# Two more seven-product pairs in the first and last feed-forward layer, and conditioning blocks placed anew

## What is computed

```python
def _swiglu(h, w13, w2):
    a, b = jnp.split(h @ w13, 2, axis=-1)
    return (jax.nn.silu(a) * b) @ w2

m = jax.nn.silu(cvec) @ ada_w[l] + ada_b[l]     # 9 vectors of D per layer
x + 0.5 * m[gate] * _swiglu(_modulate(x, m, s, g), w13, w2)
```

## Time and profile before

| | us |
|---|---|
| median of 3 runs | 3096.23 (3092.04 to 3099.06) |
| the profiled execution | 3098.46 |
| its span, first to last instruction | 3096.4 |
| PE busy / PEld busy | 2959.1 / 2722.7 |
| DVE busy / ACT busy / POOL busy | 2005.0 / 1135.8 / 275.6 |
| mean granted TensorE clock | 0.988 of full speed |

### The profile page before, as it was taken

One profiled execution on the slowest core, in us unless ns is written; L12 is line 12 of the kernel. 1 busy time (PEld: TensorE's weight loads), 2 busy tenths in 40 slices (PEclk: granted clock), 3 DMA queues, 4 the chain that ended last, 5 costly groups with the idle time before them and its releaser, 6 DMA issues.

```text
span 3096.4 us, 46067 instructions
## 1 busy us (share of the span) xinstructions
PE 2959.1 (96%) x18222; PEld 2722.7 (88%) x18222; DVE 2005.0 (65%) x3616; ACT 1135.8 (37%) x2024; POOL 275.6 (9%) x335
## 2 busy tenths in 40 slices
PE   7999999998999899999999999999999999999998
PEld 3999998988878899998999998878687886899998
DVE  3778977245756787887687766463545545667756
ACT  4223434335455233534343444222212222534433
POOL 1000002011003000003000003030301104100001
PEclk9999999999999899999999999999999999999999
DMA  5454342220101333342233222313223241122221
GB/s 220 135 176 126 107 133 90 81 70 26 41 15 62 116 123 122 107 126 94 71 116 116 91 92 89 116 64 98 96 70 122 69 135 41 41 89 89 79 80 67
DMA packets 87686, 294.42 MB, mean 95 GB/s; under 512 B 10512, under 2 KB 14896, under 8 KB 86704
## 3 DMA queue, kind: packets, MB, share of 16 engines
q1 hardware_dynamic: 80080, 269.70, 26.8%
q10 hardware_dynamic: 6176, 16.54, 1.4%
q0 software_dynamic: 1216, 5.24, 0.5%
HBM read 283.96 MB, written 7.49 MB: 94 GB/s over the span
## 4 chain that ended last, share of the span: by engine, by line
PE 84%; DVE 7%; ACT 3%; POOL 2%; issue 2%; DMA 1%; DVEq 0%; POOLq 0%; SPq 0%; ACTq 0%
PE ps L2147 24%; PE ps L2180 17%; PE ps L2313 12%; PE ps L2048 11%; PE ps L2063 7%; PE ps L2109 2%; PE ps L2585 2%; POOL tmp_q L647 2%; PE ps L2594 2%; PE ps L2370 1%; PE ps L2338 1%; DMA raw<-in_ws 1%; PE ps L2261 1%; PE ps L2573 1%; PE ps L2353 1%
## 5 line engine op out<-in xcount | busy, mean ns | idle before, releaser
L2180 PE MATMUL ps<-g,w 128*128 128x320 f32 x4224 | 625.4, 309 | 2.2 <-DVE w L1303 1.3
L2180 PEld LDWEIGHTS ps<-g,w 128*128 128x128 f32 x4224 | 620.6, 188 | 3.6 <-DVE w L1303 1.6
L2147 PE MATMUL ps<-h,w 128*128 128x320 f32 x3168 | 498.9, 312 | 43.5 <-ACT swu L950 29.2
L2147 PEld LDWEIGHTS ps<-h,w 128*128 128x128 f32 x3168 | 476.3, 190 | 49.1 <-ACT swu L950 31.6
L1303 DVE TENSOR_TENSOR w<-raw,w 128x1024 fp32r<-128x1024 f32 (+1 forms) x267 | 303.1, 1141 | 224.5 <-ACT w L798 206.9
L2313 PE MATMUL ps<-w,h 128*128 128x512 f32 x1620 | 374.5, 391 | 4.8 <-ACT rv L1239 3.1
L2147 PE MATMUL ps<-e,w 128*128 128x320 f32 x2376 | 371.8, 310 | 0.0
L2313 PEld LDWEIGHTS ps<-w,h 128*128 128x128 f32 x1620 | 302.3, 188 | 70.0 <-issue 6.8
L2147 PEld LDWEIGHTS ps<-e,w 128*128 128x128 f32 x2376 | 356.1, 189 | 0.0
L811 ACT ACTIVATE w<-w2s 128x512 fp32r<-128x512 f32 x264 | 164.1, 631 | 249.7 <-DVE w2s L1450 80.6
L2063 PE MATMUL ps<-h,w 128*128 128x320 f32 x1728 | 254.3, 309 | 0.2 <-DVE w L1303 0.2
(11 more groups left out here) (249 smaller groups left out, 3381.4 us busy)
## 6 DMA issues: line engine op xcount, KB each, us to landing
raw<-in_ws SPq DMA_DIRECT2D x303, 512.0 KB, 3.6
raw<-in_ada SPq DMA_DIRECT2D x128, 512.0 KB, 3.7
raw<-in_ws SPq DMA_DIRECT2D x96, 384.0 KB, 3.2
ada<-in_ada ACTq DMA_DIRECT2D x6, 1024.0 KB, 22.1
rst<-in_state ACTq DMA_DIRECT2D x4, 1024.0 KB, 4.8
out_new_state<-rsx ACTq DMA_DIRECT2D x8, 512.0 KB, 2.6
x<-in_xT SPq DMA_DIRECT2D x4, 640.0 KB, 8.0
ada<-in_ada POOLq DMA_DIRECT2D x2, 1024.0 KB, 16.2
```

What stands on the lines that cost most here:

```text
L2147: mm = pe.matmul(ps[:, 4 * s + bank, 0:HT], w2[:, at // 2, wi, c:c + P], rhs(k, ri), start=start and k + wi + ri == 0, stop=(k == 3 and wi ...
L2180: mm = pe.matmul(pair_half(pr, half), w2[:, slot_of(n), wi, c:c + P], half_of(g2[:, k, ri, :], half), start=k + wi + ri == 0, stop=(k == n ...
```

## The change

The number of plain pairs goes from 10 to 8 in FFN 0 and from 4 to 2 in FFN 3, and the T values of FFN 3 are made one pair earlier. The conditioning blocks are spread anew (128 in all as before, with those of the retention layer). The fourth T value gets a buffer of its own in all FFNs, so that FFN 0 uses the order of the others. In a seven-product pair ACT makes the first copy ahead of `left_high(nxt, 0)`, and DVE makes `left_first_sum` ahead of `first_half_low` and `left_low(nxt, 0)` after the conditioning blocks.

```diff
-CLASSIC = (10, 4, 4, 4)
-T_PAIR = (3, 1, 1, 1)
+CLASSIC = (8, 4, 4, 2)
+T_PAIR = (3, 1, 1, 0)
...
-ADA_UP = [[1, 3, 3, 0, 2, 3, 3, 3, 3, 0, 0, 1, 1, 0, 1, 1, 1, 0, 1, 0, 1, 0],
-          [1, 0, 3, 2, 1, 1, 1, 0, 1, 0, 1, 0, 1, 0, 1, 0, 1, 0, 1, 0, 1, 0], [0] * FT, [0] * FT]
-ADA_DN = [[6, 6, 6, 2], [6, 6, 6, 2], [6, 6, 0, 0], [0] * 4]
+ADA_UP = [[1, 3, 3, 0, 3, 2, 3, 2, 0, 1, 1, 0, 0, 1, 1, 1, 1, 0, 0, 1, 0, 0],
+          [1, 0, 3, 2, 0, 2] + [0] * 16, [1, 0, 3, 2, 0, 2] + [0] * 16, [0] * FT]
+ADA_DN = [[7, 7, 7, 3], [6, 6, 4, 0], [6, 6, 4, 0], [0] * 4]
...
+        fourth = place("fourth", 4 * HT, at=f_at + 5 * T * 4).rearrange("p (k t) -> p k t", k=4)
...
-        def fourth_value(q):
-
-            return tscr if q else e2s[:, 2, :, 0, :]
...
-            return t_first(q) + 1 + (v if q or v < 2 else 5 - v)
+            return t_first(q) + 1 + v
...
@@ ACT, first_pairs: the T values' high parts
-                    for v in range(3 if q else 2):
+                    for v in range(3):
                         t_high(q, v)
...
                 if f + 1 == CLASSIC[q] < FT:
                     t_high(q, 3)
-                    if q == 0:
-                        t_high(q, 2)
...
@@ ACT, seven_products
-                if not last:
-                    left_high(q, f + 1, n + 2, 0)
                 if u and f > CLASSIC[q]:
                     first_half_high(f - 1, u - 1)
+                if f == CLASSIC[q] + 1:
+                    act.wait_ge(t_lo, t_turn(q, 3))
                 act.wait_ge(left_free, 5 * sg + 1)
                 act.activation(swu[:, s, 0, :], ps[:, 4 * s, 0:HT], ACT.Copy).then_inc(p_copied, 1)
                 if last:
                     split_in(q, d)
+                else:
+                    left_high(q, f + 1, n + 2, 0)
                 act.wait_ge(left_free, 5 * sg + 2)
                 act.activation(swu[:, s, 1, :], ps[:, 4 * s + 2, 0:HT], ACT.Copy).then_inc(p_copied, 1)
...
@@ DVE, first_pairs: the T values' low parts (t_low(q, 2) moves from after t_low(q, 3) to T_PAIR in FFN 0)
...
@@ DVE, seven_products
                 if not last:
-                    left_low(*nxt, 0)
+                    left_first_sum(*nxt)
                 if before:
                     first_half_low(f - 1, u - 1)
-                if not last:
-                    left_first_sum(*nxt)
                 ada_blocks(ADA_UP[q][f])
                 if not last:
+                    left_low(*nxt, 0)
                     left_second_sum(*nxt)
```

More of the change, by code:

```diff
@@ L820, in t_high @@
                 act.wait_ge(t_val, t_first(q) + 1 + v)
-                if q == 0 and v == 2:
-                    act.wait_ge(t_lo, t_turn(q, 3))
                 if v < 3:
@@ L825, in t_high @@
                 else:
-                    act.activation(h2[:, 0:4, 0, HT:T], fourth_value(q), ACT.Copy).then_inc(t_hi, 1)
+                    act.activation(h2[:, 0:4, 0, HT:T], fourth, ACT.Copy).then_inc(t_hi, 1)
             def norm_sq(k, nn, ready, h=None):
@@ L1494, in t_values @@
                     low_done(dve, nn, 0, k)
-                dve.tensor_tensor(fourth_value(q), tscr, t2, ALU.subtract).then_inc(t_val, 1)
+                dve.tensor_tensor(fourth, tscr, t2, ALU.subtract).then_inc(t_val, 1)
             def t_low(q, v):
@@ L1507, in t_low @@
                 else:
-                    dve.tensor_tensor(h2[:, 0:4, 1, HT:T], fourth_value(q), h2[:, 0:4, 0, HT:T].bitcast(fp32), ALU.subtract
+                    dve.tensor_tensor(h2[:, 0:4, 1, HT:T], fourth, h2[:, 0:4, 0, HT:T].bitcast(fp32), ALU.subtract
                                       ).then_inc(t_lo, 1)
@@ L1545, in first_pairs @@
                     t_low(q, 1)
-                    if q:
-                        t_low(q, 2)
+                    t_low(q, 2)
                 if seven:
```

## The result

The changed kernel takes **3115.15 us** (median of 5 runs, 3112.75 to 3119.16) where the kernel before takes 3096.23: ratio **1.0057 [1.0046, 1.0069]**, slower by 18.9 us. The forecast was 3108.4 in a range of 3096 to 3120. The profiled execution took 3119.16 us with a span of 3117.4, 21.0 above the span before, at a mean granted clock of 0.981 (0.988 before). So kernels are compared by their medians, and places inside them by the traces.

What follows compares the result with a forecast made beforehand. PE work (busy 2959 of 3096 us) plus few stalls was taken as the bound. Terms -7.0 - 16.4 + 14.6 + 20.0 + 0.9 = +12.1 on 3098.5 gave 3110.6, less 2.2 a median of 3108.4 us; range 3096 to 3120.

Steps and rivals of the forecast that it cites:

- transition stall: PE's wait at product 3 of the first seven-product pair: FFN 2's pair 4, +12.5, and FFN 0's pair 8, +7.7.
- seventh block: Conditioning block in FFN 0's down tiles, m = 6: its late load holds DVE; pairs 12 and 18 lose +5.0 each.
- FFN 1, -16.4: FFN 1: pairs 6 to 21 lose all their blocks, pair 4 its own, the last down products two; -16.4 us in sum.
- FFN 2, +14.6: FFN 2 gets FFN 1's block pattern: pair 4 +12.5, pair 5 +0.9, the moved low part +1.2; +14.6 us in sum.
- FFN 0, pair 8, +7.7: FFN 0's first seven-product pair, now 8, repeats the stall of FFN 1's pair 4: loss 15.5 for 7.8, +7.7 us.
- The down gap, -1.6: FFN 0, pair 5 has two blocks for three: a 1.30 us wait in the down products goes, with its restart, -1.6.
- pairs 9, 10 and 13 to 16 of FFN 0, +1.9 forecast: FFN 0: a block each in pairs 9 and 10 costs +0.9, and one each in pairs 13 to 16 costs +1.0.
- DVE waits in each pair with a block: Rival, chance 0.13: the moved first sum may wait about 1 us in seven FFN 0 pairs; 3115 to 3117 us.
- The last down products of FFN 0, +2.0: FFN 0's last down products get a third block behind tile 2's add, 0 to 2.6 us, taken as +2.0.
- transition stall not back: Rival, chance 0.07: no stall at product 3 of FFN 2's pair 4 and FFN 0's pair 8, 20.2 less; 3088.2 us.
- seventh block hidden: Rival, chance 0.14: the load lands in time, FFN 0's pairs 12 and 18 stay as they are, 10.0 less; 3098.4 us.
- The fourth rival: Chance 0.02: the 48 matmuls saved are replaced by equal waits, as DVE has more to do in seven-product pairs; 3115.4 us.

Runs made afterwards that it cites:

- FFN 3's part alone: The kernel before with only FFN 3 changed: two plain pairs for four and the T values one pair earlier; 3094.44 us, ratio 0.9999.
- the last experiment: The changed kernel with six for seven blocks, both orders as before, low parts 5 and 6 ahead of blocks, ten plain pairs in FFN 0; 3078.15 us, ratio 0.9935.

## Why the prediction was right, and by how much it was off

The forecast was for slower by the coming back of the transition stall and by the seventh block, at +12.1 of trace; the trace has +21.0. Segment by segment the changed places sum to +18.7. The rest lies in places that no edit touches, most of it between FFN 2 and FFN 3: +2.8 in two stretches, of which 0.9 comes back before FFN 3 begins. Direction, range and mechanism were right. The median came 6.7 above the forecast, and one term is 9.0 too small; the others are off by 1.7 us or less each, together -2.4.

- **Four pairs, -7.0:** the matmuls went as told; the counts show it.
- **FFN 1, -16.4:** -17.2 in its pairs (rounds -1.7, -7.2, -4.7, -3.6) and -0.9 in the last down products, so -18.1. Rounds 1 to 3 came to 74.3, 74.9 and 49.3, within 1 us of 73.9, 73.9, 49.3. Pair 4 kept 14.1 of 16.8, 15.5 forecast. The copy moved ahead is not what gave more: with ACT's order as before the pair loses 14.4. With the tables of before it loses 16.7, so the whole gain goes with the new table.
- **FFN 2, +14.6:** +12.0, +0.6 and +0.2 in its rounds, +12.9. Pair 4 loses 14.4 (15.5 forecast), PE waits 12.38 there for ACT's copy as said ("12 to 13 us"), and 12.1 in pair 4 of FFN 1 and in pair 8 of FFN 0. The tables of before bring pair 4 of FFN 2 back to 2.7, and the low parts moved ahead of the blocks take 5.3 to 6.1 us off at each place: that two blocks ahead of the ring's release make the stall is shown, not only argued. How the 9 us that then stay divide between the work left ahead of low part 5 and the load's own time is read from the timeline alone.
- **FFN 0, pair 8, +7.7:** it loses 15.0 for pair 10's 7.7, so +7.3. The down gap, -1.6: it was -1.6.
- **The seventh block, +10.0:** pairs 12 and 18 lose 9.4 and 8.0 for 3.8 each, +9.8, by the chain as worked out: 3.7 from issue to use of the block, and PE 6.49 idle for 6.7 forecast (6.24 in pair 18). Taking the block out gave 12.7 in the median. Without it they lose less than the 3.8 of before, which fits with the block of their own that both pairs had then and have no more: in FFN 1 the same two pairs lose 1.0 and nothing without theirs, 4.4 and 3.6 with it.
- **The term that was too small: pairs 9, 10 and 13 to 16 of FFN 0, +1.9 forecast.** "A fourth is +1.0" took the price of such a pair from the old order. The pairs beside 8, 12 and 18 lose 12.8 for 1.9 of before, +10.9. The cost was in the text as the rival "DVE waits in each pair with a block", at about 1 us in each of seven pairs and a chance of 0.13. It should have been a term of the sum. Nothing excluded it: the prediction itself said that the load goes out only after low part 5, and put +0.6 a round on the moved low part in FFN 1 and 2, where it has no blocks to meet. What it also missed is the other half, ACT's high part behind a copy that waits for PE, which costs about the same alone. Undone together they give 8.1, and the pairs lose 4.9. The 3.0 that this is above the 1.9 of before goes with the new table, which gives four of these pairs a block that had none; it was not taken apart.
- **The last down products of FFN 0, +2.0:** +3.2 here (29.77 for 26.54). Among the nine others with the same three blocks it was 28.5 in three (+2.0), about 29.8 in five and 31.0 in one (both orders as before); why it differs is open.
- **FFN 3, +0.9:** +1.3, pair 2 loses 4.2 for 3.8 to 3.9 forecast.

The rivals "transition stall not back" and "seventh block hidden" fell by the first sight of the windows. The largest sum, 3115 to 3117, named with the DVE rival, is where the time came out. The fourth rival's 3115.4 is as near, but as the cause of the time it falls: FFN 3's part alone keeps about 2.1 of its 3.5 in the trace. In FFN 0 it holds in part, since there, by the last experiment, the two pairs bring nothing.

The estimate from the Trainium skill ("DMA: Bandwidth & Descriptors", "Anatomy of one DMA — SWDGE (gpsimd) path"), 3.2 us for 512 KB, would have put the sum 3.5 lower. The rows above have 3.5 to 3.7 from issue to use, so the trace is the better price here, as the loads go another issuing path.

## What to carry to other kernels

Where one ring of buffers feeds several engines that run their programs in order, find the operation that releases a place and look at what stands ahead of it: moving it ahead of two optional blocks at three places gave 14.3 us, while moving the waiting copies gave nothing in the median. An operation that needs a load just issued is not free to move earlier by a place, even on an engine that is 65% busy: it stops all that is behind it. And price a moved operation with the order it will stand in, not with the rows of the old one.

## What was not expected

- Two causes that hide each other. By the medians, DVE's order undone alone gave 1.7 us, ACT's alone lost 0.6, and both together gave 8.1. Either run by itself would have called the order free.
- A stall costs more than its wait. In pair 4 of FFN 2 the wait was 12.38 and the loss 14.4; the product behind it took 3.57 where 1.92 is usual, and the granted clock is 0.74 in the window of the pair:

```profile
1512.30:1539.00 26.70, 14.32 (x86) 14.06 (x85) 20.20 (x34) 10.54 (x19) 0.00 (x0) 0.74 0.23 80
```

- Short waits differ in what they bring. In FFN 0 of the changed kernel a wait of 0.65 left the next 24 matmuls at 3.78 (row above; 3.68 is usual), and one of 1.88, a pair later, was followed by 5.31 for 24, part of them at half clock (granted clock 0.67 from 372.4 to 377.6). But in the kernel before, a wait of 1.80 left the next 18 at 2.91, the full pace, so the length of the wait alone doesn't tell. The row of the 1.88:

```profile
372.47 5.31 PE L2138 MATMUL ps<-h,w 128*128 128x320 f32 x24 [1.88 <-DVE swu L1612]
```

- Open: why pair 10, with fewer blocks ahead, still loses 7.9 in the last kernel, and what of the remaining 9 us at each transition a load issued ahead of low part 5 would give. Neither was tried.
